# Engines exchanged at the first tile, eight warm-ups, and an attention bias table stored in two parts, in a hybrid attention and convolution encoder

## The reference

```python
# mixer 0: differential attention
h = rmsnorm(x, gain0) @ w_in                  # 2048 x 8192: q, k, v, gate
s = q . k (8 heads x 2 parts, 128 wide) / sqrt(128) + bias   # bias: relative position, by head
p = softmax(s); a = p[0] - lam * p[1]; o = a @ v
y = (rmsnorm_per_head(o) * (1 - lambda_init) * silu(gate)) @ w_out
# mixer 1: h = rmsnorm(x, gain1) @ w_in (2048 x 6144) + b -> a, g, z;
# u = depthwise conv, 31 taps, of a * sigmoid(g); layernorm, silu, * silu(z), @ w_out + b_out
```

## Time and profile before

| | us |
|---|---|
| median of 3 runs | 823.56 (823.46 to 823.87) |
| the profiled execution | 822.98 |
| its span, first to last instruction | 821.2 |
| TensorE matmul busy | 813.7 (99%) |
| VectorE busy | 659.9 (80%) |
| ScalarE busy | 460.6 (56%) |
| GpSimd busy | 235.9 (29%) |
| moved by DMA | 175.21 MB, mean 213 GB/s |

### The profile page before, as it was taken

How to read it: one execution, slowest core, us unless ns; L and a number is a source line. 1 busy time by engine, 2 the same in 40 slices (tenths; PEclk the granted TensorE clock), 3 DMA queues, 4 the chain that set the end, 5 groups by cost and what they waited for, 6 DMA issues and landing times.

```text
span 821.2 us, 13878 instructions
## 1 busy us (share of the span) xinstructions
PE 813.7 (99%) x5616; PEld 752.7 (92%) x5616; DVE 659.9 (80%) x1111; ACT 460.6 (56%) x600; POOL 235.9 (29%) x115
## 2 busy tenths in 40 slices
PE   9999999999999999999999999999999999999996
PEld 9988899889998899888888899999999999998885
DVE  7578784697658794698788987999999999569782
ACT  7756643547336543656554455455664555597562
POOL 0300010000000000002000008989889888680000
PEclk9999999999999999999999999999999999999999
DMA  9987599976654566534656557556556556556842
GB/s 329 392 298 273 186 268 352 329 186 205 216 192 153 172 195 219 191 114 156 218 191 205 191 173 233 189 191 205 184 179 204 175 188 203 183 209 226 307 152 102
DMA packets 104113, 175.21 MB, mean 213 GB/s; under 512 B 3792, under 2 KB 41168, under 8 KB 103512
## 3 DMA queue, kind: packets, MB, share of 16 engines
q1 hardware_dynamic: 99712, 163.65, 58.3%
q0 software_dynamic: 2720, 8.39, 4.5%
q10 hardware_dynamic: 1624, 2.38, 0.8%
HBM read 172.30 MB, written 12.08 MB: 225 GB/s over the span
## 4 chain that ended last, share of the span: by engine, by line
PE 99%; ACT 0%; issue 0%; POOL 0%; DVE 0%; POOLq 0%
PE ps_acc L1391 17%; PE ps_acc L1394 17%; PE ps_acc L1393 17%; PE ps_acc L1377 13%; PE ps_acc L1379 13%; PE ps_acc L1380 13%; PE ps_acc L1440 1%; PE ps_acc L1444 1%; PE ps_acc L1447 1%; PE ps_d L1497 1%; PE ps_a L1353 0%; PE ps_a L1490 0%; PE ps_d L1476 0%; PE ps_d L1478 0%; PE ps_a L1492 0%; PE ps_d L1477 0%
## 5 line engine op out<-in xcount | busy, mean ns | idle before, releaser
L535 ACT ACTIVATE sb_w_hi<-sb_w_raw 128x2048 fp32r<-128x2048 f32 x142 | 271.3, 1919 | 209.6 <-PE ps_acc L1394 142.6
L918 DVE TENSOR_TENSOR sb_w_lo<-sb_w_raw,sb_w_hi 128x2048 fp32r<-128x2048 f32 x97 | 220.3, 2289 | 80.6 <-ACT sb_w_hi L535 80.2
L490 POOL TENSOR_TENSOR sb_w_lo<-sb_w_raw,sb_w_hi 128x2048 fp32r<-128x2048 f32 x45 | 208.1, 4632 | 252.5 <-ACT sb_w_hi L535 252.5
L1391 PE MATMUL ps_acc<-sb_conv_hi,sb_w_hi 128*128 128x256 f32 x768 | 213.3, 278 | 0.0
L1394 PE MATMUL ps_acc<-sb_conv_hi,sb_w_lo 128*128 128x256 f32 x768 | 212.5, 277 | 0.0
L1393 PE MATMUL ps_acc<-sb_conv_lo,sb_w_hi 128*128 128x256 f32 x768 | 212.4, 277 | 0.0
L1149 DVE SCALAR_TENSOR_TENSOR ps_d<-sb_uT,sb_dwT,ps_d 128x256 f32<-128x256 f32 x480 | 188.9, 480 | 4.5 <-ACT ps_d L770 4.5
L1377 PE MATMUL ps_acc<-sb_w_hi,sb_act_hi 128*128 128x512 f32 x384 | 149.9, 390 | 0.0
L1379 PE MATMUL ps_acc<-sb_w_lo,sb_act_hi 128*128 128x512 f32 x384 | 149.7, 390 | 0.0
L1380 PE MATMUL ps_acc<-sb_w_hi,sb_act_lo 128*128 128x512 f32 x384 | 149.5, 389 | 0.0
L1393 PEld LDWEIGHTS ps_acc<-sb_conv_lo,sb_w_hi 128*128 128x128 f32 x768 | 144.3, 188 | 0.0
(11 more groups left out here) (209 smaller groups left out, 892.2 us busy)
## 6 DMA issues: line engine op xcount, KB each, us to landing
sb_w_raw<-in_attn_w_in SPq DMA_DIRECT2D x59, 1024.0 KB, 7.3
sb_w_raw<-in_conv_w_in SPq DMA_DIRECT2D x64, 512.0 KB, 4.6
sb_w_raw<-in_attn_w_out SPq DMA_DIRECT2D x16, 1024.0 KB, 5.1
sb_w_raw<-in_conv_w_in SPq DMA_DIRECT2D x16, 1024.0 KB, 5.1
sb_w_raw<-in_conv_w_out SPq DMA_DIRECT2D x15, 1024.0 KB, 5.0
weight_sums<-in_conv_w_out POOLq DMA_DIRECT2D x6, 1024.0 KB, 12.1
sb_w_raw<-weight_sums SPq DMA_DIRECT2D x4, 1024.0 KB, 5.8
sb_w_raw<-in_attn_w_in SPq DMA_DIRECT2D x15, 256.0 KB, 4.5
```

Of the source, the lines that this page charges most:

```text
L490: pool.tensor_tensor(w_part(w_lo, c), w_raw[c % RING][:], w_part(w_hi, c).bitcast(F32), ALU.subtract).then_inc(lo_ready_pool, 1)
L535: act.activation(w_part(w_hi, c if like is None else like), w_raw[slot][:], ACT.Copy).then_inc(hi_ready, 1)
L918: dve.tensor_tensor(w_part(w_lo, like), w_raw[slot][:], w_part(w_hi, like).bitcast(F32), ALU.subtract).then_inc(lo_ready, 1)
L1391: pe.matmul(into, left_hi, hi[:, kt], start=(kt == 0 and f % 2 == 0), stop=False, skip_group_check=True)
```

## The change

At the first piece the engines change places: VectorE makes x's high part (`first_x_hi`), ScalarE the high part of the first half of the weights; VectorE still makes the second half. All other high parts of x stay ScalarE's, so that their semaphore counts one less everywhere. There are eight warm-ups. Chunk 7's high part moves on ScalarE ahead of the wait for the mean, the root and q's high part, and its low part on VectorE ahead of q's low part. The bias table is stored in two DMAs, heads 0 and 1 at slot 4 and heads 2 to 7 at slot 8 of pair 0, where ScalarE's queue first waits until the first part is stored. The sync queue waits for the first part behind the load of chunk 11 instead of chunk 13 and loads pair 0's bias there; in the later pairs it waits for both parts.

```diff
-WARM_UP = 9
+WARM_UP = 8
@@ sync queue, load_pair
-                        if (t, i) == ((3, 1) if first else (0, NCH - 1)):
+                        if (t, i) == ((2, NCH - 1) if first else (0, NCH - 1)):
                             if first:
                                 sp.wait_ge(windows_stored, 16)
                             else:
+                                sp.wait_ge(windows_stored, 32)
                                 sp.wait_ge(max_ready, 4 * j)
@@ ScalarE, first piece
+                if p == 0:
+                    act.wait_ge(piece_landed(0), 16)
+                    act.activation(w_part(w_hi, slot)[:, rows, 0:GC], w_raw[slot][:, rows, 0:GC], ACT.Copy
+                                   ).then_inc(first_hi, 1)
+                    act.wait_ge(x_landed[0], 16)
+                    continue
@@ ScalarE, after the squares
+            high_part(RING + 3, 3, 2)
             act.wait_ge(ms_ready, 1)
             act.activation(sd, ms, ACT.Sqrt).then_inc(sd_ready, 1)
@@ ScalarE
+            def store_windows(first, upto):
+
+                act.wait_ge(line_stored, 16)
+                if first:
+                    act.wait_ge(windows_stored, 16)
+                act.dma_start(windows_dram[first:upto], bass.AP(line_dram.tensor, line_dram.offset + P - 1 + first * REL,
+                                                                [[REL, upto - first], [-1, P], [1, BW]])
+                              ).then_inc(windows_stored, 16)
...
                 if i == 4 and type(j) is int and j == 0:
-                    act.wait_ge(line_stored, 16)
-                    act.dma_start(windows_dram, bass.AP(line_dram.tensor, line_dram.offset + P - 1,
-                                                       [[REL, HEADS], [-1, P], [1, BW]])).then_inc(windows_stored, 16)
+                    store_windows(0, 2)
+                if i == 8 and type(j) is int and j == 0:
+                    store_windows(2, HEADS)
...
             high_of_q(0)
-            high_part(RING + 3, 3, 2)
@@ VectorE, first piece
-                    dve.wait_ge(piece_landed(0), 16)
-                    dve.tensor_copy(w_part(w_hi, slot)[:, rows, 0:GC], w_raw[slot][:, rows, 0:GC]).then_inc(first_hi, 1)
+                    dve.wait_ge(x_landed[0], 16)
+                    dve.tensor_scalar(act_hi[:, 0], xT[:, 0], gain_in[:, 0:1], None, ALU.mult).then_inc(first_x_hi, 1)
                     dve.wait_ge(rest_landed, 16)
-                    dve.tensor_copy(w_part(w_hi, slot)[:, rows, GC:], w_raw[slot][:, rows, GC:]).then_inc(first_hi, 1)
+                    dve.tensor_copy(w_part(w_hi, slot)[:, rows, GC:], w_raw[slot][:, rows, GC:]).then_inc(first_rest, 1)
@@ VectorE, pair_slot
+                if i == 3 and type(j) is int and j == 0:
+                    low_part(RING + 3, 3)
                 if i == 3:
                     for f in range(2):
                         dve.wait_ge(q_hi_ready, 2 * j + f + 1)
@@ TensorE, head_slot
-                    pe.wait_ge(split_hi, kt + 1)
+                    if p:
+                        pe.wait_ge(split_hi, kt)
+                    else:
+                        pe.wait_ge(first_x_hi, 1)
...
-                            pe.wait_ge(first_hi, 2)
+                            pe.wait_ge(first_rest, 1)
```

More of the change, by code:

```diff
@@ L201, in build @@
         first_hi, head_hi, head_lo = sem("first_hi"), sem("head_hi"), sem("head_lo")
+        first_x_hi, first_rest = sem("first_x_hi"), sem("first_rest")
         rest_landed = sem("rest_landed")
@@ L557, in _ @@
                                    ).then_inc(split_hi, 1)
-                if p:
-                    act.wait_ge(piece_landed(p), 16)
-                    act.activation(w_part(w_hi, slot)[:, rows], w_raw[slot][:, rows], ACT.Copy
-                                   ).then_inc(hi_ready if closes else head_hi, 1)
+                act.wait_ge(piece_landed(p), 16)
+                act.activation(w_part(w_hi, slot)[:, rows], w_raw[slot][:, rows], ACT.Copy
+                               ).then_inc(hi_ready if closes else head_hi, 1)
             act.wait_ge(vecs_landed, 16)
@@ L935, in _ @@
                 if p == 0:
-                    dve.wait_ge(piece_landed(0), 16)
-                    dve.tensor_copy(w_part(w_hi, slot)[:, rows, 0:GC], w_raw[slot][:, rows, 0:GC]).then_inc(first_hi, 1)
+                    dve.wait_ge(x_landed[0], 16)
+                    dve.tensor_scalar(act_hi[:, 0], xT[:, 0], gain_in[:, 0:1], None, ALU.mult).then_inc(first_x_hi, 1)
                     dve.wait_ge(rest_landed, 16)
-                    dve.tensor_copy(w_part(w_hi, slot)[:, rows, GC:], w_raw[slot][:, rows, GC:]).then_inc(first_hi, 1)
+                    dve.tensor_copy(w_part(w_hi, slot)[:, rows, GC:], w_raw[slot][:, rows, GC:]).then_inc(first_rest, 1)
                 dve.wait_ge(x_landed[p], 16)
                 for kt in range(k0, k1):
-                    dve.wait_ge(split_hi, kt + 1)
+                    if p:
+                        dve.wait_ge(split_hi, kt)
+                    else:
+                        dve.wait_ge(first_x_hi, 1)
                     dve.scalar_tensor_tensor(act_lo[:, kt], xT[:, kt], gain_in[:, kt:kt + 1],
@@ L946, in _ @@
                 if p == 0:
-                    dve.wait_ge(first_hi, 2)
+                    dve.wait_ge(first_hi, 1)
+                    dve.wait_ge(first_rest, 1)
                 elif closes:
@@ L1055, in pair_slot @@
                                 ALU.mult, ALU.mult).then_inc(m_ready, 1)
-                if not by_pool(16 * j + i + RING):
+                if (type(j) is not int or (j, i) != (0, 3)) and not by_pool(16 * j + i + RING):
                     low_part(16 * j + i + RING, i % NCH, pair_chunk(j, i + RING))
@@ L1085, in m_low @@
                 for kt in range(4 * n, 4 * n + 4):
-                    dve.wait_ge(split_hi, KT + kt + 1)
+                    dve.wait_ge(split_hi, KT + kt)
                     dve.scalar_tensor_tensor(act_lo[:, kt], mT[:, kt], vecs[:, G_HEAD, kt:kt + 1],
@@ L1111, in x1_low @@
                 for kt in range(4 * n, 4 * n + 4):
-                    dve.wait_ge(split_hi, 2 * KT + kt + 1)
+                    dve.wait_ge(split_hi, 2 * KT + kt)
                     dve.scalar_tensor_tensor(conv_lo[:, kt], x1T[:, kt], vecs[:, G_CONV, kt:kt + 1],
```

## The result

| | before | after |
|---|---|---|
| median of six runs each, side by side | 823.71 (823.04 to 825.28) | 829.97 (829.51 to 830.75) |
| ratio, 95% interval | | 1.0072 [1.0059, 1.0085] |
| the profiled execution | 822.98 | 829.67 |
| its span | 821.2 | 827.9 |
| TensorE matmul busy | 813.7 | 815.6 |

The kernel is slower by 6.3 us. The chain that ended last (the page, part 4) shows what was not in it before: transfers.

The account below looks back on a forecast made before the run. TensorE was taken to bound the kernel (99% of the chain). Start -0.2, chunk 7 +0.2 and pair 0's attention +4.8 on 822.98 gave 827.8, median 828.4 (0.6 above); range 822.9 to 830.0, the forecast's own 825.5 to 830.0.

Parts of the forecast that it names:

- What bounds, and where: First 95 us: TensorE holds 99% of the chain; beyond the warm-up, places where it stands or waits hold some 0.5 us.
- Start, -0.2: Kernel start: one warm-up fewer and engines exchanged move the first weight load from 4.80 to 4.37, gaining 0.2 us.
- Chunk 7, 0: Switch to the eighth chunk: reordering worth 0 (bounds -0.1 to +0.1); low part at 41.6, TensorE waits 0.4 us, not 0.2.
- Where the first part sits: Bias store, pair 0: two heads sit on two engines, so the first part takes as long as the whole, landing at 55.7.
- Chunk 12, 64.0: Attention of pair 0: chunk 12 lands at 64.0 against 57.65, so the scores start at 68.2, 4.8 us late.
- the sum: Whole kernel: start -0.2, chunk 7 +0.2, attention of pair 0 +4.8 on 822.98 give a profiled execution of 827.8.
- ScalarE's exponentials, no extra: Attention of pair 0: chunks 13 and 14 go ahead of the exponentials; no extra, up to 0.5 us if they come later.
- (a): Rival at the bias store: first part spread over four engines or more, so not slower, 823.2 or 823.3; chance 23%.
- (b): Rival at the bias store: first part overtakes the loads and lands at 52 to 54, 823.4 to 825.5; chance 6%.
- (c): Rival at chunk 12: six-head part halves the loads' pace fully, chunks 13 and 14 add to it, 830 to 833; chance 8%.

Follow-up runs that it names:

- start alone: The kernel before with only the start changed (eight warm-ups, engines exchanged at the first tiles): 823.86, ratio 1.0004.
- the spread kernel: The kernel after, two parts and waits kept, with the line stored in eight shifted copies per head so the store uses all 16 engines: 822.96, ratio 0.9991.
- the late part: The kernel after with the second part (six heads) issued at slot 13 instead of slot 8 of pair 0: 827.08, ratio 1.0032.
- the swapped bias: The kernel after with the bias load issued behind chunk 12's load instead of ahead of it: 829.22, ratio 1.0070.
- the parts alone: The kernel before with only the two-part store and its waits; start and chunk 7 as before: 830.26, ratio 1.0081.
- the second part of two heads: The kernel after with three parts: two heads at slot 4, two at slot 8, four at slot 13: 829.84, ratio 1.0072.
- four heads first: The kernel after with four heads in each part instead of two and six: 830.25, ratio 1.0077.
- the wait behind chunk 13: The kernel after with the sync queue's wait put back behind chunk 13's load, the two parts kept: 824.98, ratio 1.0019.

## Why the prediction held, step by step

The forecast was 828.4 and 829.97 came, 0.03 us inside the range that ends at 830.0; three of the six runs lie above it. The sign, the place and the mechanism held and one term was too small; that the number still fell into the range is luck.

**What bounds, and where.** Held: TensorE's chain; the loss lies at the two stops that were named, the score banks and a x v (3.60 + 1.30 us), and in the half clock between them, which was not named.

**Start, -0.2.** The engines did what was said (x 0.35 us, half tile 0.42, first load at 4.37), the gain didn't come. The step that failed is the one that let the pace rise at 5.6 again: it rose at 6.2, so the two slow matmuls that went were replaced by others, and the second piece starts at 6.62 instead of 6.58. Over all kernels the granted clock rose anywhere between 4.2 and 7.2 with eight warm-ups and between 4.4 and 6.4 with nine; a difference of 0.2 us can't be forecast from one trace of it. The second half of that step held: what is won there is lost at chunk 7 (start alone, 0.57 us of idleness).

**Chunk 7, 0.** Nothing speaks against it, though the time (0.9995 [0.9986, 1.0004]) can't tell the stated 0.1 us. The low part came at 41.23, not 41.6, because the chunk landed at 37.3 instead of 37.7; the chain behind it (1.92 + 1.53 + 0.4) was right. The wait of 0.4 us that I forecast was none. In the three kernels without the reordering TensorE's weight loads stood there for 0.20 to 0.58 us, in those with it for 0 to 0.26. That is no gain of the reordering: the two stops of 0.57 and 0.58 belong to the two kernels whose clock rose first (4.2 and 4.4), so that TensorE came early, and chunk 7's first weight load comes at 43.98 to 44.27 without it and at 43.8 to 44.6 with it.

**Where the first part sits.** Held, and it is the step that carries the case. Two landing records for two heads, six for six; 0.12 of the engines; bias issue at 55.59 against 55.7. That it fits to 0.1 us is luck: in the other kernels with the same first part and the wait behind chunk 11 the part was stored at 55.0 to 56.8. And the store was issued at 37.49, 1.1 us sooner than before, where I had reckoned that it comes later beside the root. What the step was worked out from is in the trace of before: eight landings for the store's 1536 KB in eight heads, 57.4 to 60.3, so 192 KB each, and eight of chunk 12's sixteen shares at 56.9 to 57.6 where the other eight were there by 52.9. Over all kernels a store of 8, 2, 6 or 4 heads landed in 8, 2, 6 or 4 shares, and the spread store, in 16, 48 or 64 blocks of 16 rows, in 16.

**Chunk 12, 64.0.** This is the term that was mis-sized: 65.94. Without the second part beside it, 61.8 was forecast and 61.68 measured. With it I added 1.8 to 2.7, from the distance of two loads beside the store of before; measured are 4.25. Counted from its own issue chunk 12 took 4.4 us longer than without the part. By the estimate above, what was left out is that the second part first ran at 117 GB/s for 2 us, 20 of 24 for each of its six engines, before it fell to 62. From the landing to the scores the forecast held (4.2 us against 4.16), so the scores came at 70.10 instead of 68.2, and 1.9 us is the whole difference between the profiled 829.67 and the 827.8 of the sum.

**ScalarE's exponentials, no extra.** Held: VectorE has one gap of 0.70 us between 70.10 and 97.25, as before.

**The rivals.** (a), four engines or more, is the spread kernel: it took 822.96, where 823.0 to 823.3 was worked out for it. That is 0.9 us below the kernel before beside it, where the rival had 0.3 to 0.6. (b) needs a first part that overtakes; none did. (c) is nearest to the time, and its mechanism (the full halving) nearer than my own choice of 1.8 to 2.7; but chunks 13 and 14 did not add to it as it says. The clock fell too, which no case had. In after that costs nothing: TensorE still waits 1.30 us for VectorE at the end of the stage, and at full clock it would have waited longer; in the kernels with the late part and with the swapped bias, where it falls behind the last stop, it does.

## What to carry to other kernels

Before splitting a DMA, count in the trace how many shares it lands in. Here the store and its parts landed in one share for each head, so the part of two heads took about as long as the whole (18.1 us against 21.7, with two loads fewer on its engines), and chunk 12 beside it was landed only with its late shares (in after 65.2 to 65.9, the first ones at 61.1). A wait moved forward on an in-order queue is paid by all that is issued behind it: chunk 12 was issued at 56.0 instead of 46.15, and here the queue's own loads (5 us) cost more than the wait saved. If a store must be there sooner, spread it first: here the whole one, landed in 16 shares, was through at 52.1 instead of 60.3, and the split was not needed (822.77, with the split 822.96).

## What the runs showed of the hardware

- The second part on ScalarE's queue, issued at 55.65 and 55.67, moved its first bytes at 57.8 in after, where the sync queue had the 384 KB bias ahead (landed at 58.2 to 58.7), and at 59.8 with the bias behind chunk 12, where it had a 1 MB chunk ahead (60.1 to 61.0). In after it then ran at 117 GB/s in six shares for 2 us before it fell to 62; with the chunk ahead it began at some 75.
- After TensorE had stood still the granted clock was 0.50 to 0.52 for 3.4 us: after 3.60 us in the kernel after, 2.65 with the parts alone, 3.62 with the second part of two heads, 2.21 and 4.70 ahead of a x v. After 3.10 us with four heads first it was so for 6.8 us. After the 1.66 us in the profiled execution with the wait behind chunk 13 it stayed at 1.00. The fall came between 0.2 and 2.3 us after the work had started again, but with the bias behind chunk 12 0.4 us ahead of that, in the stop itself. Where TensorE sets the end (the late part), fifteen matmuls at 0.21 instead of 0.11 us cost 1.5 us.
- The pace of weight loads and matmuls at the start doubled at very different moments: with nine warm-ups between 4.4 and 6.4 us, with eight between 4.2 and 7.2, in kernels whose start is the same. What decides on it stays open.
